# Adding the residual on POOL instead of VectorE at three normalised borders of a two-block fp32 kernel

## The chip, the core and the metric

The kernel runs on one core of one Trainium2 chip. The metric is the device time of one execution, in microseconds (us). TensorE is called PE here, its weight loads PEld, VectorE is DVE, ScalarE is ACT, GpSimd is POOL, and SyncE (SP) issues the DMAs.

## What is computed

`x` is 512 tokens of 1024 features in float32. The first block is a feed-forward, an attention mixture and a second feed-forward; each of them ends with a norm of its output and a residual add. A second block of two hybrid layers follows.

```python
def _rmsnorm(x, g):
    xf = x.astype(jnp.float32)
    r = lax.rsqrt(jnp.mean(xf * xf, axis=-1, keepdims=True) + EPS)
    return (xf * r * g.astype(jnp.float32)).astype(x.dtype)

# first_block
f = _swiglu(_rmsnorm(x, ffn1_pre_g[l]), ffn1_w_gate[l], ffn1_w_up[l], ffn1_w_down[l])
x = x + 0.5 * _rmsnorm(f, ffn1_post_g[l])            # border 1
h = _rmsnorm(x, mix_pre_g[l])
...
x = x + _rmsnorm(heads @ w_out[l], mix_post_g[l])    # border 2
f = _swiglu(_rmsnorm(x, ffn2_pre_g[l]), ffn2_w_gate[l], ffn2_w_up[l], ffn2_w_down[l])
x = x + 0.5 * _rmsnorm(f, ffn2_post_g[l])            # border 3
```

## The kernel before

The 512 tokens are four chunks of 128 tokens (`NC = 4`), one token per partition. Every matmul is done in three fp32r passes: each operand is split into a high part and a low part, and PE multiplies high by high, high by low and low by high (lines 1287 to 1289). Weights come as 326 slabs plus 8 extra ones, of 128 x 1024 floats each. A slab is loaded by SP, ACT casts it to its high part (`highs`, line 549), and POOL subtracts that from the raw slab to get the low part (`lows`, line 510, which writes `w_lo` or, for the extra slots, `x_lo`). PE waits for that low part before it uses a slab.

Between two stages stands a border. Border 1 lies between the first feed-forward and the qkv projection, border 2 between the mixture's output projection and the second feed-forward, border 3 between the second feed-forward and the first hybrid layer. At each of these three, and for each chunk `c` in turn, the two engines ACT and DVE hand the work to and fro:

- ACT squares and sums the product `f` of the chunk, which lies in two PSUM banks (`norm_f`, lines 555 and 556). DVE adds the two sums (line 858), ACT takes the root (line 559), DVE the reciprocal (line 860).
- DVE scales `f` by that and by the gain `g_post` into `xn` (line 867, two instructions, `new_x`), and adds `xn` to `x_tok` in place (line 870). That add raises `x_done`.
- ACT squares and sums the new `x_tok` (`norm_x`, line 569, which waits for `x_done`) and takes the root (line 570). DVE takes the reciprocal (line 881) and scales `x_tok` by it and by `g_pre` into `xn` (line 888, `normed`), which raises `xn_ready`.
- PE transposes `xn` (`turn_chunk`, line 1281). ACT copies the high part of the transposed chunk (`take_high`, line 576), DVE subtracts to get the low part (`take_low`, line 896), which raises `xtl_done`; then PE may multiply with that chunk.

Each engine's order is written out by hand and is strict. On DVE it is `new_x(c)`, `normed(c)`, `take_low(c-1)`; on ACT `norm_f(c)`, `norm_x(c)`, `take_high(c-1)`. Between `norm_x(0)` and `norm_f(1)` ACT casts two slabs of the next stage, those in the extra slots, and POOL makes their low parts. POOL has nothing else to do from there to the end of the border.

On PE the sums of the stage before end chunk by chunk (`out_product`), with the transposes of chunks 0 and 1 set after the sums of chunks 2 and 3. At borders 1 and 3 the next stage begins with `chunk_group`: for each chunk PE waits for `xtl_done` of this chunk, does 24 matmuls, and for the first two chunks then transposes chunk `c + 2`. At border 2 the next stage is `ffn`: its first matmuls wait for `xtl_done` of two chunks at once, then the transposes of chunks 2 and 3 come, and then a second wait for the other two chunks.

Of the kernel before, what the change touches and what calls it, by code (L numbers as in the profile page):

```python
# [8 lines left out]
ALU = mybir.AluOpType  # L9
# [8 lines left out]
NC = SEQ // P  # L18
# [7 lines left out]
LEAD = 4  # L26
# [15 lines left out]
S_QKV = N_IN + N_DOWN  # L42
S_OUT1 = S_QKV + N_QKV
# [79 lines left out]
def build(nc, x, ffn1_pre_g, ffn1_post_g, ffn1_w_gate, ffn1_w_up, ffn1_w_down, mix_pre_g, mix_post_g,  # L123
# [4 lines left out]
    with ExitStack() as ctx:  # L128
# [11 lines left out]
        def put(name, shape, dtype=F32):  # L140
            t = at(name, shape, dtype, place[0])
            place[0] += size(shape, dtype)
            assert place[0] <= arena_base + arena, (name, place[0] - arena_base - arena)
            return t


        x_tok = put("x_tok", [NC, D])
# [23 lines left out]
        xn = put("xn", [2, D])  # L171
# [78 lines left out]
        def f32(t):  # L250

            return t.bitcast(F32)
# [16 lines left out]
        def inv_sum(c):  # L269
            return col(96 + c)  # L270
# [13 lines left out]
        def factor2(par, comp=0, n=1):  # L284
            return col(114 + 2 * par + comp, n)
# [5 lines left out]
        def sem(name):  # L291
            return ctx.enter_context(nc.semaphore(name))
# [13 lines left out]
        acc_done = sem("acc_done")  # L306
        sqf_done, ssf_done, rtf_done = sem("sqf_done"), sem("ssf_done"), sem("rtf_done")
        x_done = sem("x_done")
        rtx_done = sem("rtx_done")
        xn_ready = sem("xn_ready")  # L310
        tr_done = sem("tr_done")
# [33 lines left out]
        def cols(c, n=P):  # L345
            return slice(c * n, (c + 1) * n)
# [4 lines left out]
        def stage_end(b):  # L351

            return {1: S_QKV, 2: S_FFN[1], 3: S_LAYER0, 4: S_LAYER0 + N_LAYER, 5: N_SLABS}[b]

        def wait_chunk_sums(eng, b, c):

            if c < NC - 1:
                eng.wait_ge(acc_done, 3 * (b - 1) + c + 1)
            else:
                eng.wait_ge(w_used, stage_end(b))  # L360

        def layer_start(l):
            return S_LAYER0 + l * N_LAYER
# [134 lines left out]
        @block.gpsimd  # L498
        def _(pool):
            pool.memset(ident[:, :], 0.0).then_inc(pool_step, 1)  # L500
            pool.wait_ge(pool_step, 1)
            pool.affine_select(out=ident[:, :], in_=ident[:, :], compare_op=ALU.not_equal, fill=1.0, base=0,
                               pattern=[[-1, P]], channel_multiplier=1).then_inc(ident_ready, 1)

            def lows(a, b):

                for s in range(a, b):
                    pool.wait_ge(hi_ready, s + 1)
                    i = slot_of[s]
                    pool.tensor_tensor(lo_slots[i], raw_slots[i], f32(hi_slots[i]), ALU.subtract).then_inc(lo_ready, 1)  # L510


            lows(0, S_OUT1 + LEAD)
            for i in range(16 * NC):
                pool.wait_ge(rd_done, i + 1)
                p = p_tok[:, i % NC, :]
                pool.tensor_scalar(p, p, inv_sum(i % NC), 1.0, ALU.mult, ALU.mult).then_inc(pn_done, 1)  # L517
            done = S_OUT1 + LEAD
            for l in range(LAYERS):
                upto = layer_start(l) + N_PROJ_A + LEAD  # L520
                lows(done, upto)
                done = upto
                for i in range(16):
                    n = 16 * l + i
                    w = (i % NC + 1) * P
                    pool.wait_ge(c2_done, n + 1)
                    p = p2[:, 2 * (n % 2), 0:w]
                    pool.tensor_scalar(p, p, factor2(n % 2), 1.0, ALU.mult, ALU.mult).then_inc(pw_done, 1)
            lows(done, N_SLABS)
# [314 lines left out]
        def _(dve):  # L844
            steps = [0]

            def link(ins):

                steps[0] += 1
                ins.then_inc(dve_step, 1)  # L850
                dve.wait_ge(dve_step, steps[0])

            def new_x(b, c):

                if b in (1, 2, 3):
                    n = 4 * (b - 1) + c + 1
                    dve.wait_ge(sqf_done, n)
                    dve.tensor_tensor(ss_f, ss_a, ss_b, ALU.add).then_inc(ssf_done, 1)
                    dve.wait_ge(rtf_done, n)
                    link(dve.reciprocal(inv_f, root_f))  # L860
                    if c == 0:
                        dve.wait_ge(post_in, 16 * b)
                    if 4 * b + c >= 2:
                        dve.wait_ge(tr_done, 4 * b + c - 1 if c >= 2 else 4 * b)
                    for half, bk in enumerate((bank[4 + c], bank[c])):
                        sl = cols(half, 512)
                        ins = dve.scalar_tensor_tensor(out=xn[:, c % 2, sl], in0=bk[:, :], scalar=inv_f,
                                                       in1=g_post[:, sl], op0=ALU.mult, op1=ALU.mult)
                    link(ins)
                    dve.tensor_tensor(x_tok[:, c, :], x_tok[:, c, :], xn[:, c % 2, :], ALU.add).then_inc(x_done, 1)  # L870
                elif b >= 4:
                    wait_chunk_sums(dve, b, c)
                    for half, bk in enumerate((bank[4 + c], bank[c])):
                        sl = cols(half, 512)
                        ins = dve.tensor_tensor(x_tok[:, c, sl], bk[:, :], x_tok[:, c, sl], ALU.add)  # L875
                    ins.then_inc(x_done, 1)
# [23 lines left out]
            def boundary(b):  # L900
                for c in range(NC):
                    new_x(b, c)
                    normed(b, c)
                    if c >= 1 and b < 5:
                        take_low(b, c - 1)
                if b < 5:
                    take_low(b, NC - 1)
# [85 lines left out]
            for c in range(NC):  # L993
                dve.wait_ge(qkv_evac, 16 + c + 1)
                ins = dve.tensor_tensor(v_hilo[:, c, 2:10, HD:P], bank[c][:, :].rearrange("p (h d) -> p h d", d=HD),
                                        f32(v_hilo[:, c, 2:10, 0:HD]), ALU.subtract)
# [77 lines left out]
            for l in range(LAYERS):  # L1074
# [60 lines left out]
                for i in range(17):  # L1135
                    n = 16 * l + i
                    h, c = i // NC, i % NC
# [86 lines left out]
                s = layer_start(l) + N_PROJ_A + N_PROJ_B  # L1224
# [20 lines left out]
                for jj in range(4):  # L1245
                    for b in range(3):
# [4 lines left out]
                        for jh in range(2):  # L1251
# [7 lines left out]
                            else:  # L1259
                                dve.tensor_tensor(m_tmp[:, :], src, g, ALU.mult).then_inc(gm_done, 1)  # L1260
                                dve.wait_ge(gm_done, 2 * n + jh + 1)
                                ins = dve.tensor_tensor(m_sum[:, jh, :], m_sum[:, jh, :], m_tmp[:, :], ALU.add)  # L1262
# [391 lines left out]
```

## Time and profile before

| | us |
|---|---|
| median of 3 runs | 2571.01 |
| lowest and highest of them | 2568.86, 2574.23 |
| the profiled execution | 2573.89 |
| its span in the profile | 2572.1 |
| PE busy in the span | 2303.0 (90%) |
| DVE busy | 762.4 (30%) |
| ACT busy | 801.3 (31%) |
| POOL busy | 870.3 (34%) |

The profiled execution is 2.88 us above the median and inside the spread of the others, so a difference worked out from its rows can be added to the median. PE is nearly full over the span; the other three engines are at a third. What an engine's operation is worth is thus decided by the few places at which PE waits for it.

### The profile page before, as it was taken

To read this page: it belongs to the slowest core of one execution; us is meant where nothing else is said; L and a number is where in the kernel's file an instruction comes from. 1 tells how busy PE (TensorE), PEld (TensorE's weight loads), DVE (VectorE), ACT (ScalarE), POOL (GpSimd) and SP (SyncE) were. 2 spreads that over 40 slices of the span, in tenths; PEclk is the share of its full clock that TensorE was granted. 3 is DMA by queue.
4 is the path that set the end of the run, shared out by engine and by line. 5 is a ranking of instruction groups with operands and counts; after the bars stand their busy time and mean duration, and the time that the engine had idled before them with its cause. 6 is when DMAs were issued, how large, how long until landed. Compare 5 with 4: busy or idle time off the path is not lost. (4 is left out here: it accounts for less than half of the span.)

```text
span 2572.1 us, 24728 instructions
## 1 busy us (share of the span) xinstructions
PE 2303.0 (90%) x10064; PEld 1873.7 (73%) x10064; DVE 762.4 (30%) x1411; ACT 801.3 (31%) x1391; POOL 870.3 (34%) x436
## 2 busy tenths in 40 slices
PE   5999999877667999999968879999997698799998
PEld 5888888755446888887747767888785587688886
DVE  2111006955653211103244333212124342331112
ACT  3222224244334322213334222222233332323222
POOL 3444443421113344443403303444442041144441
PEclk9999999966769999999957959999997597699999
DMA  4333333300002333322202202333231031033331
GB/s 139 98 94 95 98 107 116 90 1 0 1 1 65 91 99 98 98 92 97 86 1 75 89 1 78 94 98 98 82 111 33 33 91 41 25 99 94 95 98 66
DMA packets 231536, 190.94 MB, mean 74 GB/s; under 512 B 6400, under 2 KB 192256, under 8 KB 231168
## 3 DMA queue, kind: packets, MB, share of 16 engines
q1 hardware_dynamic: 231424, 189.37, 24.3%
q8 instruction: 80, 1.31, 0.2%
q14 instruction: 32, 0.26, 0.0%
HBM read 187.25 MB, written 2.10 MB: 74 GB/s over the span
## 5 line engine op out<-in xcount | busy, mean ns | idle before, releaser
L510 POOL TENSOR_TENSOR w_lo<-w_raw,w_hi 128x1024 fp32r<-128x1024 f32 x326 | 787.9, 2430 | 1245.3 <-ACT w_hi L549 1244.7
L1287 PE MATMUL bank<-xt_hi,w_hi 128*128 128x512 f32 (+1 forms) x1376 | 531.3, 386 | 17.9 <-DVE xt_lo L896 14.9
L1288 PE MATMUL bank<-xt_lo,w_hi 128*128 128x512 f32 (+1 forms) x1376 | 530.3, 385 | 0.0
L1289 PE MATMUL bank<-xt_hi,w_lo 128*128 128x512 f32 (+1 forms) x1376 | 529.6, 385 | 0.0
L549 ACT ACTIVATE w_hi<-w_raw 128x1024 fp32r<-128x1024 f32 x326 | 341.5, 1056 | 454.8 <-DMA w_raw<-in_w_in 203.9
L1287 PEld LDWEIGHTS bank<-xt_hi,w_hi 128*128 128x128 f32 x1376 | 263.1, 191 | 70.5 <-DVE xt_lo L896 16.0
L1288 PEld LDWEIGHTS bank<-xt_lo,w_hi 128*128 128x128 f32 x1376 | 263.2, 191 | 50.3
L1289 PEld LDWEIGHTS bank<-xt_hi,w_lo 128*128 128x128 f32 x1376 | 263.0, 191 | 50.4
L1287 PE MATMUL bank<-w_hi,xt_hi 128*128 128x512 f32 (+1 forms) x624 | 243.6, 390 | 4.1 <-DVE xt_lo L1042 2.8
L1288 PE MATMUL bank<-w_lo,xt_hi 128*128 128x512 f32 (+1 forms) x624 | 241.9, 388 | 0.0
L1289 PE MATMUL bank<-w_hi,xt_lo 128*128 128x512 f32 (+1 forms) x624 | 241.7, 387 | 0.0
L923 DVE TENSOR_TENSOR h_raw<-bank,act_gate 128x512 f32<-128x512 f32 x44 | 30.4, 692 | 399.9 <-PE bank L1289 399.9
L1287 PEld LDWEIGHTS bank<-w_hi,xt_hi 128*128 128x128 f32 x624 | 118.9, 190 | 29.7 <-DVE xt_lo L1042 3.2
L1288 PE MATMUL bank<-w_lo,h_hi 128*128 128x512 f32 x352 | 138.6, 394 | 0.0
L1287 PE MATMUL bank<-w_hi,h_hi 128*128 128x512 f32 x352 | 138.1, 392 | 0.0
L1289 PE MATMUL bank<-w_hi,h_lo 128*128 128x512 f32 x352 | 136.7, 388 | 0.0
L1289 PEld LDWEIGHTS bank<-w_hi,xt_lo 128*128 128x128 f32 x624 | 118.7, 190 | 23.9
L1288 PEld LDWEIGHTS bank<-w_lo,xt_hi 128*128 128x128 f32 x624 | 118.9, 191 | 23.3
L607 ACT ACTIVATE act_gate<-bank 128x512 f32<-128x512 f32 x44 | 26.3, 598 | 325.1 <-PE bank L1289 325.1
L517 POOL TENSOR_SCALAR p_tok<-p_tok,stat 128x512 f32<-128x512 f32 x64 | 44.3, 692 | 223.0 <-DVE stat L1015 222.7
L1287 PE MATMUL bank<-k_hi,q_hi 64*128 64x512 f32 (+3 forms) x128 | 59.6, 620 | 50.2 <-DVE k_lo L1004 30.4
L833 ACT ACTIVATE gate_sb<-bank 128x512 f32<-128x512 f32 x48 | 28.7, 598 | 198.6 <-PE bank L1289 198.6
(210 smaller groups left out, 3150.9 us busy)
## 6 DMA issues: line engine op xcount, KB each, us to landing
w_raw<-in_w_in SPq DMA_DIRECT2D x132, 512.0 KB, 3.8
w_raw<-in_ffn_w_down SPq DMA_DIRECT2D x44, 512.0 KB, 3.6
w_raw<-in_ffn_w_gate SPq DMA_DIRECT2D x43, 512.0 KB, 3.9
w_raw<-in_ffn_w_up SPq DMA_DIRECT2D x43, 512.0 KB, 3.8
w_raw<-in_w_out SPq DMA_DIRECT2D x24, 512.0 KB, 3.6
w_raw<-in_w_branch SPq DMA_DIRECT2D x24, 512.0 KB, 3.4
w_raw<-in_w_qkv SPq DMA_DIRECT2D x16, 512.0 KB, 3.8
x_tok<-in_x SPq DMA_DIRECT2D x4, 512.0 KB, 7.4
```

The lines of the kernel that those rows point to most:

```text
L510: pool.tensor_tensor(lo_slots[i], raw_slots[i], f32(hi_slots[i]), ALU.subtract).then_inc(lo_ready, 1)
L517: pool.tensor_scalar(p, p, inv_sum(i % NC), 1.0, ALU.mult, ALU.mult).then_inc(pn_done, 1)
L549: act.activation(hi_slots[i], raw_slots[i], ACT.Copy).then_inc(hi_ready, 1)
L607: act.activation(act_gate[:, f % 2, :], bank[gate_up_banks(f)[0]][:, :], ACT.Silu)\
L833: act.activation(gate_sb[:, jh, :], bank[b4 + jh][:, :], ACT.Sigmoid).then_inc(gs_done, 1)
L923: dve.tensor_tensor(h_raw[:, f % 2, :], bank[gate_up_banks(f)[1]][:, :], act_gate[:, f % 2, :], ALU.mult).then_inc(h_done, 1)
L1287: pe.matmul(out_ap, ah, bh, start=first, stop=False)
L1288: pe.matmul(out_ap, ah, bl, start=False, stop=False)
L1289: return pe.matmul(out_ap, al, bh, start=False, stop=last)
```

## The change

The residual add of borders 1, 2 and 3 goes from DVE to POOL. DVE's second scaling instruction (line 867) now raises a new semaphore `f_scaled`, in place of the link to the add behind it; POOL waits for `f_scaled`, adds, and raises `x_done`, for which ACT waits as before. In POOL's order the add of chunk 0 stands after the low parts of the first two slabs of the next stage, then come the low parts of the next two slabs (those in the extra slots), then the adds of chunks 1 to 3, and then the remaining low parts. The borders of the second block (`b >= 4`) are left alone.

```diff
+            def residual(b):
+
+                s = stage_end(b)
+                for c in range(NC):
+                    pool.wait_ge(f_scaled, 4 * (b - 1) + c + 1)
+                    pool.tensor_tensor(x_tok[:, c, :], x_tok[:, c, :], xn[:, c % 2, :], ALU.add).then_inc(x_done, 1)
+                    if c == 0:
+                        lows(s + 2, s + 4)
+
-            lows(0, S_OUT1 + LEAD)
+            lows(0, S_QKV + 2)
+            residual(1)
+            lows(S_QKV + 4, S_OUT1 + LEAD)
...
             done = S_OUT1 + LEAD
+            for b in (2, 3):
+                lows(done, stage_end(b) + 2)
+                residual(b)
+                done = stage_end(b) + 4
...
-                    link(ins)
-                    dve.tensor_tensor(x_tok[:, c, :], x_tok[:, c, :], xn[:, c % 2, :], ALU.add).then_inc(x_done, 1)
+                    ins.then_inc(f_scaled, 1)
```

The order of POOL around border 1, before. `w_lo` and `x_lo` are low parts of slabs, `p_tok` is the mixture's softmax:

```order
L510 TENSOR_TENSOR w_lo<-w_raw,w_hi 128x1024 [waits hi_ready] x68
L510 TENSOR_TENSOR x_lo_116<-x_raw_115,x_hi_117 128x1024 [waits hi_ready]
L510 TENSOR_TENSOR x_lo_119<-x_raw_118,x_hi_120 128x1024 [waits hi_ready]
L510 TENSOR_TENSOR w_lo<-w_raw,w_hi 128x1024 [waits hi_ready] x18
L517 TENSOR_SCALAR p_tok<-p_tok,stat 128x512 [waits rd_done] x64
```

The same place now:

```order
L511 TENSOR_TENSOR w_lo<-w_raw,w_hi 128x1024 [waits hi_ready] x68
L519 TENSOR_TENSOR x_tok<-x_tok,xn 128x1024 [waits f_scaled]
L511 TENSOR_TENSOR x_lo_116<-x_raw_115,x_hi_117 128x1024 [waits hi_ready]
L511 TENSOR_TENSOR x_lo_119<-x_raw_118,x_hi_120 128x1024 [waits hi_ready]
L519 TENSOR_TENSOR x_tok<-x_tok,xn 128x1024 [waits f_scaled] x3
L511 TENSOR_TENSOR w_lo<-w_raw,w_hi 128x1024 [waits hi_ready] x18
```

One add stands ahead of the two extra slabs and three behind them; the low parts keep their order among themselves.

The order of DVE at border 1, chunk 0 and the first steps of chunk 1, before:

```order
L858 TENSOR_TENSOR stat<-stat 128x1 [waits sqf_done]
L860 RECIPROCAL stat<-stat 128x1 [waits rtf_done]
L867 SCALAR_TENSOR_TENSOR xn<-bank,stat,g_post 128x512 [waits tr_done,post_in,dve_step]
L867 SCALAR_TENSOR_TENSOR xn<-bank,stat,g_post 128x512
L870 TENSOR_TENSOR x_tok<-x_tok,xn 128x1024 [waits dve_step]
L881 RECIPROCAL stat<-stat 128x1 [waits rtx_done]
L888 SCALAR_TENSOR_TENSOR xn<-x_tok,stat,g_pre 128x1024 [waits pre_in,dve_step]
```

The same place now:

```order
L874 TENSOR_TENSOR stat<-stat 128x1 [waits sqf_done]
L876 RECIPROCAL stat<-stat 128x1 [waits rtf_done]
L883 SCALAR_TENSOR_TENSOR xn<-bank,stat,g_post 128x512 [waits tr_done,post_in,dve_step]
L883 SCALAR_TENSOR_TENSOR xn<-bank,stat,g_post 128x512
L896 RECIPROCAL stat<-stat 128x1 [waits rtx_done]
L903 SCALAR_TENSOR_TENSOR xn<-x_tok,stat,g_pre 128x1024 [waits pre_in,dve_step]
```

The add is gone from DVE and nothing is put in its place: the next instruction after the scaling is still the reciprocal that waits for `rtx_done`. ACT, PE and SP keep their instructions and their order.

## Rows read from the trace of the kernel before

**Rows 1.** Timeline of DVE, border 1, chunk 2: start, duration, line, shapes [idle before]
```profile
401.14 1.41 DVE L867 SCALAR_TENSOR_TENSOR xn<-bank,stat,g_post 128x512 f32<-128x512 f32 x2
402.59 1.23 DVE L870 TENSOR_TENSOR x_tok<-x_tok,xn 128x1024 f32<-128x1024 f32 x1
...
405.47 1.28 DVE L888 SCALAR_TENSOR_TENSOR xn<-x_tok,stat,g_pre 128x1024 f32<-128x1024 f32 x1
406.67 1.28 DVE L896 TENSOR_TENSOR xt_lo<-bank,xt_hi 128x512 fp32r<-128x512 f32 x2
...
408.49 1.41 DVE L867 SCALAR_TENSOR_TENSOR xn<-bank,stat,g_post 128x512 f32<-128x512 f32 x2
```

**Rows 2.** Timeline of ACT, border 1, the same chunk
```profile
403.85 1.06 ACT L569 ACTIVATE junk<-x_tok 128x1024 bf16<-128x1024 f32 x1 [2.94 <-DVE x_tok L870]
...
405.03 0.20 ACT L570 ACTIVATE stat<-stat 128x1 f32<-128x1 f32 x1
```

**Rows 3.** Timelines of PE's weight loads and matmuls, border 1 (PEld) and both borders (PE)
```profile
399.47 0.86 PEld L1281 LDWEIGHTS bank<-ident,xn 128*128 128x128 f32 x8 [0.53 <-DVE xn L888]
400.66 0.19 PEld L1287 LDWEIGHTS bank<-w_hi,xt_hi 128*128 128x128 f32 x1 [0.34 <-DVE xt_lo L896]
406.80 0.85 PEld L1281 LDWEIGHTS bank<-ident,xn 128*128 128x128 f32 x8 [0.76 <-DVE xn L888]
...
414.15 1.09 PE L1281 MATMUL bank<-ident,xn 128*128 128x128 f32 x8 [0.32 <-DVE xn L888]
...
1220.59 1.09 PE L1281 MATMUL bank<-ident,xn 128*128 128x128 f32 x8 [0.32 <-DVE xn L888]
```

**Rows 4.** One line of the source each: durations in ns, least, median, most
```profile
L870 DVE TENSOR_TENSOR x_tok<-x_tok,xn x12: 1224/1225/1514, 386.6 to 1216.4; 128x1024 f32<-128x1024 f32 x12
...
L510 POOL TENSOR_TENSOR w_lo<-w_raw,w_hi x326: 2332/2402/2944, 11.0 to 2536.7; 128x1024 fp32r<-128x1024 f32 x163
...
L517 POOL TENSOR_SCALAR p_tok<-p_tok,stat x64: 691/691/696, 519.4 to 766.6; 128x512 f32<-128x512 f32 x64
```

**Rows 5.** Timelines in the mixture: DVE releases POOL; POOL's work; PEld released by POOL
```profile
702.66 0.16 DVE L1015 RECIPROCAL stat<-stat 128x1 f32<-128x1 f32 x1
...
702.92 0.69 POOL L517 TENSOR_SCALAR p_tok<-p_tok,stat 128x512 f32<-128x512 f32 x1 [10.33 <-DVE stat L1015]
...
522.60 0.69 POOL L517 TENSOR_SCALAR p_tok<-p_tok,stat 128x512 f32<-128x512 f32 x1 [0.59 <-DVE stat L1015]
...
523.65 0.71 PEld L1281 LDWEIGHTS bank<-ident,p_tok 128*128 128x128 f32 x4 [0.65 <-POOL p_tok L517]
```

**Rows 6.** Timelines of POOL, DVE and ACT, border 1, chunk 1
```profile
390.30 5.09 POOL L510 TENSOR_TENSOR x_lo<-x_raw,x_hi 128x1024 fp32r<-128x1024 f32 x2 [6.50 <-ACT x_hi L549]
417.39 5.21 POOL L510 TENSOR_TENSOR w_lo<-w_raw,w_hi 128x1024 fp32r<-128x1024 f32 x2 [22.00 <-ACT w_hi L549]
...
394.98 1.50 DVE L870 TENSOR_TENSOR x_tok<-x_tok,xn 128x1024 f32<-128x1024 f32 x1
...
396.51 1.06 ACT L569 ACTIVATE junk<-x_tok 128x1024 bf16<-128x1024 f32 x1 [3.21 <-DVE x_tok L870]
```

**Rows 7.** Timeline of PE, border 2
```profile
827.89 1.09 PE L1281 MATMUL bank<-ident,xn 128*128 128x128 f32 x8 [0.25 <-DVE xn L888]
836.42 0.58 PE L1287 MATMUL bank<-xt_hi,w_hi 128*128 128x256 f32 x1 [7.44 <-DVE xt_lo L896]
...
850.18 1.04 PE L1281 MATMUL bank<-ident,xn 128*128 128x128 f32 x8
853.72 0.58 PE L1287 MATMUL bank<-xt_hi,w_hi 128*128 128x256 f32 x1 [2.50 <-DVE xt_lo L896]
```

**Rows 8.** Stretches at border 2: length, then busy us of PE, PEld, DVE, ACT, POOL, granted clock, DMA
```profile
834.00:836.00 2.00, 0.00 (x0) 0.00 (x0) 2.00 (x3) 1.89 (x6) 0.00 (x0) 0.50 0.00 0
838.00:840.00 2.00, 2.00 (x13) 2.00 (x12) 1.53 (x2) 0.40 (x1) 0.00 (x0) 0.61 0.00 0
854.00:856.00 2.00, 2.00 (x10) 2.00 (x11) 0.00 (x0) 0.00 (x0) 0.00 (x0) 0.50 0.00 0
```

More of the change, by code:

```diff
@@ L308, in build @@
         x_done = sem("x_done")
+        f_scaled = sem("f_scaled")
         rtx_done = sem("rtx_done")
```

## The prediction

> **What bounds the kernel now.** I read the page first: PE is busy 90% of the span, so an operation of another engine costs only where PE waits for it. Then I read the timelines of the four engines over the three borders that the change touches. At border 1 the reader should follow one chunk round. DVE scales the product (401.14, 1.41 us) and adds it to x (402.59, 1.23 us) [rows 1]; 0.03 us later ACT squares the new x (403.85) and takes the root (405.03) [rows 2]; DVE makes xn (405.47, 1.28 us) and the low part of the chunk before (406.67, 1.28 us), and starts to scale the next chunk at 408.49 [rows 1]. That is a round of 408.49 - 401.14 = 7.35 us in which no two of the steps overlap. DVE sits in an ordered queue and can't use the time while ACT works. PE is a little faster than this round: its weight loads stand idle 0.53, 0.34 and 0.76 us for xn or for the low part, and the transposes of the last chunk still wait 0.32 us for xn, at border 3 as at border 1 [rows 3]. So at these borders the round of ACT and DVE sets the end, and PE has no spare time in front of it that could hide a longer round. At border 2 it is plainer: PE stands 7.44 us for the low part of chunk 1 and later 2.50 us for that of chunk 3 [rows 7].
>
> The add is a link of that round. It is 1.23 us between the scaling and ACT's squares, and all twelve adds take this except one of each border (1224 ns least, 1225 median, 1514 most) [rows 4].
>
> **What the change takes away.** From the end of the scaling (401.14 + 1.41 = 402.55) to the start of ACT's squares (403.85) the link is 1.30 us [rows 1, 2]. DVE has nothing to do with the time it is given: its next instruction waits for the root that ACT takes after the add. The freed DVE time is therefore worth nothing.
>
> **What it adds.** The same link is now: DVE releases POOL, POOL adds, POOL releases ACT.
>
> - DVE to POOL: a reciprocal ends at 702.66 + 0.16 = 702.82 and POOL starts at 702.92, after 10.33 us of idleness, so 0.10 us [rows 5].
> - The add. No row has POOL adding two float32 tiles. The nearest is its subtraction on the same 128x1024 shape with two float32 inputs: 2402 ns median, 2332 least [rows 4]. The far bound is its one-input operation, 691 ns on 512 elements, or 1.38 us on 1024 [rows 4]. I take 2.40, since the add has two inputs and the same size.
> - POOL to ACT: no row shows it. Bounds are the 0.03 us from DVE to ACT [rows 1, 2] and the only row in which an engine was released by POOL, PEld at 523.65 after a POOL operation that ended at 522.60 + 0.69 = 523.29, so 0.36 us at most [rows 5]. I take 0.10, as for the release in the other direction.
>
> Sum 0.10 + 2.40 + 0.10 = 2.60 us against 1.30, so **1.30 us more** for each of chunks 0, 2 and 3. POOL is idle there: it stands 22.00 us between the extra slabs and the next one [rows 6].
>
> The Trainium skill, GPSIMD Engine Reference, section "Performance versus the Vector engine", gives about 2.6 cycles per element for an elementwise operation of two inputs; at 1.2 GHz an estimate from that page for 1024 elements is 2.2 us, not 2.40. By the page the whole sum below would be about 2 us smaller. The rows of POOL's own subtraction decide here.
>
> Chunk 1 differs, because the two extra slabs stand ahead of it in POOL's queue. Before, POOL worked on them until 390.30 + 5.09 = 395.39, DVE's add (394.98) took 1.50 instead of 1.23 beside it, and ACT started at 396.51 [rows 6]. The slabs start from the same point of ACT's work as before, so in this chunk's own time they still end at 395.39; the scaling ended at about 394.94 and its release would reach POOL by 395.04, so the add starts at 395.39 and ACT at 395.39 + 2.40 + 0.10 = 397.89. That is **1.38 us more**. Behind the adds of chunks 1 to 3 in POOL's queue stand the low parts of the next slabs, and they wait for nothing new: their casts come on ACT only after its last step of the border.
>
> **What of it reaches the end.** Borders 1 and 3: the last wait of PE there is for xn of chunk 3, behind all four rounds [rows 3]. Delay 3 x 1.30 + 1.38 = 5.28 us each. Behind it PE does 24 matmuls and needs chunk 3's low part only at their end, which comes as far ahead as before. Border 2: the long wait ends with the low part of chunk 1, which DVE makes only after xn of chunk 2; so three rounds are in it, 2 x 1.30 + 1.38 = 3.98 us. The fourth is hidden: xn of chunk 3 is transposed at 850.18 behind work of PE without a wait, and the 2.50 us after that are counted from this transposition, so they stay [rows 7].
>
> Total 5.28 + 3.98 + 5.28 = 14.5 us. Slabs, casts, low parts and DMAs of the following stages are released by PE or come after the border on their engines, so everything behind moves as a block, and nothing there is late that was not.
>
> **PE's clock.** It falls to 0.50 in the 7.44 us wait and is 0.61 at 838 to 840, after which PE is at full clock; in the 2.50 us wait it falls again and is 0.50 at 854 to 856 [rows 8]. These are the two levels 1.2 and 2.4 GHz. About 2.8 us of PE's work ran at the low one after the first wait (836.42 to about 839.2), which cost some 1.4 us. Now the same wait is longer, and it costs that anyway. At borders 1 and 3 the wait for xn of chunk 1 grows from 0.53 to 0.53 + 1.30 + 1.38 = 3.2 us, more than the 2.50 that sufficed at border 2, so the clock may fall there. But each following round of PE now has 1.3 us to spare against the longer round of the others, which takes up most of such a 1.4 us. I put nothing into the sum and 0 to 1.4 us per border into the range.
>
> Against the profiled execution's 2573.89 us this is 2588.4; that execution lies 2.9 us above the median, so against the median 2571.01 it is 2585.5. **Forecast 2585.5 us**, 0.56% slower. The bounds of the unknowns: POOL's release at 0.03 or at 0.36 us moves it by 11 x -0.07 = -0.8 or 11 x 0.26 = +2.9 us; the add at its least, 2332 ns, by -0.8; the clock by up to +4.2; the scatter of the runs by about 2 either way.
>
> **Rivals.**
>
> 1. The add at POOL's one-input pace. If a plain float32 add ran at 1.38 us [rows 4] rather than 2.40, a round would grow by 0.28 instead of 1.30, and chunk 1 by 0.36: 2 x 1.20 + 0.92 = 3.3 us, 2574.3 us, within 0.2% and so not slower by what can be told. It decides from an add of about 1.6 us down; below 1.1 us (1.30 less the two releases) the kernel would even become faster. For it: nothing but the missing row. Against it: the subtraction reads the same two kinds of input. Chance 0.05, of which 0.01 for faster.
> 2. A low clock at borders 1 and 3 that isn't taken up, for instance because it falls in the last waits, behind which no wait of PE is left, or because border 2 starts longer at 1.2 GHz than before. Price 1.4 us each at three or four places, with the forecast's 14.5: 2589 to 2592, say 2590. For it: the clock fell after 2.50 us of waiting [rows 8]. Against: at border 1 waits of 0.3 to 0.8 us did not pull it down, and the new ones after chunk 1 are 1.6 to 2.1 us. Chance 0.15.
> 3. The delay is hidden, in that PE's waits of 0.3 us at borders 1 and 3 are only the edge of the record and PE itself is the limit with 1 us to spare per round. Then only 0.3 of each 1.3 us would count there: about 3 + 4 = 7 us, 2578 us. Against it: PE's waits repeat in each round, each named as waiting for DVE. Chance 0.05.
>
> **How the numbers follow.** Forecast with its own range 2581 to 2589: 0.75. Rival 1: 0.05, rival 2: 0.15, rival 3: 0.05. A measurement of this kernel can tell about 0.2%, 5 us, from no change. Slower by more: 0.95; within: 0.04, which is rival 1; faster: 0.01. The range reaches over rival 2: 2580 to 2592 us.
>
> **What would show it.** In the profile of the changed kernel: POOL's adds at 2.4 us, ACT's idle time before its squares at about 4.2 us instead of 2.94, a round of 8.65 us instead of 7.35, PE's wait before the second transposes of border 1 at about 3.2 us and before the later ones at about 1.6 to 2.1, the long wait of border 2 at 7.44 + 1.3 = 8.7 us (the rest of its 3.98 stands before the transposes). The stage behind each border should be as long as before. An add under 2 us, or a round still at 7.4 us, would refute the first step; a PE that doesn't wait longer would refute the second; a stage behind the border that is shorter or longer would mean that I missed what moves with it.

## The result

The changed kernel takes 2586.73 us (median of 5 runs, 2586.30 to 2587.95); the kernel before, now with five runs, 2573.24 us (2568.86 to 2575.41). The ratio is **1.0056**, with a 95% interval of 1.0041 to 1.0070: slower by 13.5 us from median to median, by some 11 to 18 us by the interval. The profiled execution of after took 2586.73 us with a span of 2584.9.

The line of the page after with the busy time of each engine answers to the table of before:

```profile
PE 2304.6 (89%) x10064; PEld 1873.9 (72%) x10064; DVE 746.8 (29%) x1399; ACT 801.2 (31%) x1391; POOL 898.2 (35%) x448
```

DVE loses 12 instructions and 15.6 us, POOL gains 12 and 27.9 us, and PE does the same work in a longer span.

The line of the new add in the source view (durations in ns, least, median, most; below it, who waited for whom, in us and times) answers to [rows 4]:

```profile
L519 POOL TENSOR_TENSOR x_tok<-x_tok,xn x12: 2337/2392/2409, 386.3 to 1228.4; 128x1024 f32<-128x1024 f32 x12
...
  DVE xn L883: 45.2, 9
...
  ACT junk L585: 50.8, 12
```

The add costs 2.39 us on POOL, and ACT waits for all twelve, 50.8 us together; it was 36.1 us for DVE's.

The timeline of chunk 2 of border 1, DVE, POOL and ACT, answers to [rows 1, 2]:

```profile
403.32 1.41 DVE L883 SCALAR_TENSOR_TENSOR xn<-bank,stat,g_post 128x512 f32<-128x512 f32 x2
...
408.64 0.16 DVE L896 RECIPROCAL stat<-stat 128x1 f32<-128x1 f32 x1 [3.91 <-ACT stat L586]
...
411.86 1.41 DVE L883 SCALAR_TENSOR_TENSOR xn<-bank,stat,g_post 128x512 f32<-128x512 f32 x2
...
404.81 2.38 POOL L519 TENSOR_TENSOR x_tok<-x_tok,xn 128x1024 f32<-128x1024 f32 x1 [6.16 <-DVE xn L883]
...
407.22 1.06 ACT L585 ACTIVATE junk<-x_tok 128x1024 bf16<-128x1024 f32 x1 [4.14 <-POOL x_tok L519]
```

Read it in order of time. DVE's scaling ends at 404.73 and POOL starts at 404.81, 0.08 us later. POOL ends at 407.19 and ACT starts at 407.22, 0.03 us later. The link is 2.49 us where it was 1.30, and the round is 411.86 - 403.32 = 8.54 us where it was 7.35. DVE meanwhile stands idle 3.91 us: the time it was given is spent waiting.

PEld (first line) and PE at borders 1 and 2 answer to [rows 3, 7]:

```profile
401.64 1.42 PEld L1296 LDWEIGHTS bank<-ident,xn 128*128 128x128 f32 x8 [3.04 <-DVE xn L903]
...
401.64 1.82 PE L1296 MATMUL bank<-ident,xn 128*128 128x128 f32 x8 [2.61 <-DVE xn L903]
410.18 1.10 PE L1296 MATMUL bank<-ident,xn 128*128 128x128 f32 x8 [0.27 <-DVE xn L903]
...
418.73 1.09 PE L1296 MATMUL bank<-ident,xn 128*128 128x128 f32 x8 [1.51 <-DVE xn L903]
...
846.07 0.58 PE L1302 MATMUL bank<-xt_hi,w_hi 128*128 128x256 f32 x1 [8.60 <-DVE xt_lo L911]
...
863.26 0.39 PE L1302 MATMUL bank<-xt_hi,w_hi 128*128 128x256 f32 x1 [2.50 <-DVE xt_lo L911]
```

PE's wait before the second transposes of border 1 is 2.61 us, before the last 1.51, and the long wait of border 2 is 8.60 instead of 7.44. The 3.2 us forecast for the first of them started from the 0.53 us of PEld, and PEld's wait is 3.04; PE itself had a gap of only 0.10 us there before, which its rows don't list as a wait.

The timelines give the length of each stretch between two events. At borders 1 and 3 I take it from the scaling of chunk 0 (the start of DVE's first scaling) to PE's transposes of chunk 3, at border 2 from the same scaling to PE's first matmul behind the long wait. In the kernel before these are 414.15 - 385.18 = 28.97, 836.42 - 813.59 = 22.83 and 1220.59 - 1191.63 = 28.96 us.

| stretch of the profiled execution | before | after | difference |
|---|---|---|---|
| start to border 1 | 385.18 | 384.84 | -0.34 |
| border 1 | 28.97 | 33.89 | +4.92 |
| qkv and mixture | 399.44 | 400.89 | +1.45 |
| border 2 | 22.83 | 26.45 | +3.62 |
| rest of border 2, second feed-forward | 355.21 | 353.84 | -1.37 |
| border 3 | 28.96 | 33.90 | +4.94 |
| rest of the span | 1351.51 | 1351.09 | -0.42 |
| span | 2572.1 | 2584.9 | +12.8 |

The three borders take 13.48 us more; everything else together changes by -0.7 us. That the medians differ by the same 13.5 us is partly chance, since their interval is some 7 us wide; the borders are the surer figure.

### The profile page after: what moved, and what is told of

It reads as the page before. It is cut to its first block and busy times, and to the rows that moved or that the text cites. A ratio compares the mean times of both kernels' runs of the same rounds, so it can differ in the third digit from the quotient of the medians.

```text
span 2584.9 us, 24728 instructions
## 1 busy us (share of the span) xinstructions
PE 2304.6 (89%) x10064; PEld 1873.9 (72%) x10064; DVE 746.8 (29%) x1399; ACT 801.2 (31%) x1391; POOL 898.2 (35%) x448
```

## The experiments

Nine runs of seven kernels. The sum of the three border stretches is the finer measure: it repeats from execution to execution within 0.05 us where a border is left alone, while single executions of one kernel differ by over 10 us. Each run shared its chip with runs of the kernel before.

| run | ratio to before (95%) | border 1 | border 2 | border 3 | sum of the three, against before |
|---|---|---|---|---|---|
| before | | 28.97 | 22.83 | 28.96 | |
| the change | 1.0056 (1.0041 to 1.0070) | 33.89 | 26.45 | 33.90 | +13.48 |
| POOL at border 2 only | 1.0017 (1.0002 to 1.0032) | 28.96 | 26.43 | 28.97 | +3.60 |
| POOL at borders 1 and 3 only | 1.0050 (1.0032 to 1.0068) | 33.87 | 22.83 | 33.90 | +9.84 |
| longer link on DVE | 1.0062 (1.0044 to 1.0081) | 33.78 | 26.35 | 33.78 | +13.15 |
| no add | 0.9968 (0.9955 to 0.9980) | 26.87 | 18.76 | 26.86 | -8.27 |
| DVE adds, early parts | 0.9985 (0.9972 to 0.9999) | 27.20 | 18.70 | 27.22 | -7.64 |
| the same again | 0.9979 (0.9968 to 0.9989) | 27.19 | 18.69 | 27.19 | -7.69 |
| POOL adds, early parts | 1.0011 (0.9995 to 1.0027) | 31.51 | 20.35 | 31.51 | +2.61 |
| shared add | 1.0032 (1.0018 to 1.0045) | 29.66 | 23.45 | 29.62 | +1.97 |
| the same again | 1.0014 (1.0003 to 1.0025) | 29.64 | 23.45 | 29.64 | +1.97 |

### One part of the change at a time

```diff
             for b in (2, 3):          # border 2 only: (2,), and border 1 as before
-                    ins.then_inc(f_scaled, 1)
+                    if b in (2,):     # the other kernel: (1, 3)
+                        ins.then_inc(f_scaled, 1)
+                    else:
+                        link(ins)
+                        dve.tensor_tensor(x_tok[:, c, :], x_tok[:, c, :], xn[:, c % 2, :], ALU.add).then_inc(x_done, 1)
```

> POOL adds the residual at border 2 only; at borders 1 and 3 VectorE adds as before. My theory (each add lengthens its round by about 1.2 us, chunk 1's by 1.3, and PE's long wait of border 2 has three rounds in it): 3.7 us over the kernel before, ratio 1.0014, PE's wait after the transposes of chunk 1 at border 2 near 8.6 us, borders 1 and 3 unchanged (28.97 us from the scaling of chunk 0 to the transposes of chunk 3). Rival (all four adds of a border count, wherever they stand): 4.9 us, a third of the whole change's 13.5.

> POOL adds at borders 1 and 3 only. My theory: 4 rounds each, 3 x 1.20 + 1.30 = 4.9 us per border, 9.8 us over the kernel before, ratio 1.0038; with the kernel that has only border 2 changed it sums to the 13.5 us of the whole change. Rival (the fall of PE's clock at borders 1 and 3 costs time of its own): the two parts don't sum, or these two borders take over 5.5 us each. Rival (the clock spells of the attention stages are dealt anew): any sum, with no pattern by border.

Border 2 alone costs 3.60 us, borders 1 and 3 alone 4.90 and 4.94; the sum, 13.44, is that of the whole change (13.48), and the borders left alone keep their length to 0.01 us. The rival of four counted adds at border 2 (4.9 us) is out by the stretch, though not by the time: 1.0017 has 1.0019 in its interval. The excesses of the two ratios sum to 0.0067, and their intervals leave room for the 0.0056 of the whole change.

### A longer link without POOL

```diff
                     link(ins)
+                    for half, bk in enumerate((bank[4 + c], bank[c])):
+                        sl = slice(512 * half, 512 * half + 432)
+                        ins = dve.scalar_tensor_tensor(out=xn[:, c % 2, sl], in0=bk[:, 0:432], scalar=inv_f,
+                                                       in1=g_post[:, sl], op0=ALU.mult, op1=ALU.mult)
+                    link(ins)
                     dve.tensor_tensor(x_tok[:, c, :], x_tok[:, c, :], xn[:, c % 2, :], ALU.add).then_inc(x_done, 1)
```

> The kernel before, with VectorE's add kept, and 2 x 432 columns of the scaling done a second time in front of it (same values), which makes the same link about 1.2 to 1.25 us longer with POOL out of it. My theory (only the length of the round counts, not who adds): 4 x 1.23, 3 x 1.23, 4 x 1.23 = 13.5 us over the kernel before, the same time as the changed kernel within 0.1%. Rival (part of the cost is POOL's own: its queue, its releases, its hold on what VectorE shares with it): clearly less, 8 us or under.

DVE at border 1, the first scalings of chunks 2 and 3:

```profile
403.65 1.41 DVE L867 SCALAR_TENSOR_TENSOR xn<-bank,stat,g_post 128x512 f32<-128x512 f32 x2
...
412.27 1.41 DVE L867 SCALAR_TENSOR_TENSOR xn<-bank,stat,g_post 128x512 f32<-128x512 f32 x2
```

This is a round of 8.62 us with DVE alone, against 8.54 with POOL. The borders are 13.15 us longer, of the 13.5 expected, and the time is 1.0062, beside 1.0056 of the change. Chunk 1 accounts for what is missing: its round grew by 1.00 us and the others by 1.27, because the add there now comes behind POOL's two slabs and takes 1.22 us, not 1.50. It is the length of the link that costs, not the engine that holds it. The rival (8 us or less) falls. PE's clock fell here too, to a mean of 0.70 from 404 to 408, after a wait of 2.36 us; so that fall isn't POOL's doing either.

### How far PE is behind

```diff
-                    link(ins)
-                    dve.tensor_tensor(x_tok[:, c, :], x_tok[:, c, :], xn[:, c % 2, :], ALU.add).then_inc(x_done, 1)
+                    ins.then_inc(x_done, 1)
```

> The residual add of borders 1 to 3 is left out (x stays what it was); the scaling releases ScalarE's squares. The link loses 1.26 us per chunk. My theory (PE is just behind the round and becomes the limit at borders 1 and 3, where it needs 24 matmuls and the transposes, about 6.6 us against a round of 6.1): 1.6 us gained at each of borders 1 and 3 and 3.8 at border 2, 7 us in all, ratio 0.9973. Rival (PE is far from the limit): 5.0 + 3.8 + 5.0 = 13.8 us gained, ratio 0.9946. Rival (PE already limits at borders 1 and 3): 3.8 us, ratio 0.9985.

This kernel leaves the add out altogether. The timeline of DVE has the round at 6.07 us now, that of PE (lower two lines) has the transposes 6.41 us apart and without a wait:

```profile
397.06 1.41 DVE L867 SCALAR_TENSOR_TENSOR xn<-bank,stat,g_post 128x512 f32<-128x512 f32 x2
...
403.13 1.41 DVE L867 SCALAR_TENSOR_TENSOR xn<-bank,stat,g_post 128x512 f32<-128x512 f32 x2
...
404.34 1.04 PE L1280 MATMUL bank<-ident,xn 128*128 128x128 f32 x8
410.75 1.03 PE L1280 MATMUL bank<-ident,xn 128*128 128x128 f32 x8
```

Borders 1 and 3 gain 2.10 each and border 2 gains 4.07, 8.27 together; I had expected 1.6 and 3.8. Both rivals fall: neither is PE the limit already nor far from it. It is 7.35 - 6.41 = 0.94 us per round behind the round of the others. That is the asymmetry at borders 1 and 3: what lengthens the round counts in full, what shortens it counts for 0.94 us a round at most.

### Using DVE's idle time by another order

The chunk before is finished earlier: ACT copies its high part before it waits for the new x, and DVE subtracts its low part while ACT squares. The same lines stand in ACT's `boundary` with `take_high` and `norm_x`.

```diff
                     new_x(b, c)
+                    early = b in (1, 2, 3) and c >= 1 and (b, c) != (2, 3)
+                    if early:
+                        take_low(b, c - 1)
                     normed(b, c)
-                    if c >= 1 and b < 5:
+                    if c >= 1 and b < 5 and not early:
                         take_low(b, c - 1)
```

> The kernel before (VectorE adds), with the high and low parts of chunk c-1 taken earlier in chunk c: ScalarE's copy stands before its squares of the new x instead of behind them, VectorE's subtraction between the add and the reciprocal (chunk 3 of border 2 excepted). It then runs while VectorE waits 1.45 us for ScalarE. My theory (VectorE's idle time in a round is only worth something if a step of the round is moved into it): the round falls by 1.2 us to under PE's 6.4, so PE limits borders 1 and 3 (1.8 us gained each), and the low part that ends the long wait of border 2 comes 4.0 us sooner. Together 7.6 us under the kernel before, ratio 0.997. Rival (the two engines have no gap that fits, so the steps only change places): no change, 1.000.

The timeline of DVE, border 1, chunk 2 (starts and durations as above):

```profile
399.28 1.41 DVE L870 SCALAR_TENSOR_TENSOR xn<-bank,stat,g_post 128x512 f32<-128x512 f32 x2
400.72 1.23 DVE L873 TENSOR_TENSOR x_tok<-x_tok,xn 128x1024 f32<-128x1024 f32 x1
401.86 1.28 DVE L899 TENSOR_TENSOR xt_lo<-bank,xt_hi 128x512 fp32r<-128x512 f32 x2
403.40 0.16 DVE L884 RECIPROCAL stat<-stat 128x1 f32<-128x1 f32 x1 [0.25 <-ACT stat L570]
...
405.42 1.41 DVE L870 SCALAR_TENSOR_TENSOR xn<-bank,stat,g_post 128x512 f32<-128x512 f32 x2
```

DVE's idle time before the reciprocal falls from 1.45 to 0.25 us, since the subtraction lies in it, and the round from 7.35 to 6.14. The borders gain 7.64 us, of the 7.6 expected. The time showed less, 0.9985 (4 us), hence a second measurement:

> The early parts with VectorE adding once more. Its borders were 1.77, 4.13 and 1.75 us shorter, 7.65 us together (ratio 0.997); the time measured was 0.9985 (0.9972 to 0.9999). If the borders' gain reaches the end, the ratio comes back between 0.9965 and 0.9985 with the borders as before; if part of it is given back in a later stage, the ratio stays near 0.9985 and that stage is longer in the profile.

It gave 0.9979 (0.9968 to 0.9989) with the same stretches, -7.69. The stage between borders 2 and 3 is 1186.15 - 830.60 = 355.55 us against 355.21 before, so nothing is given back there. The interval takes in the 7.7 us of the borders (0.9970). This kernel beats both: it is some 5 us faster than the one before by the medians (4.8 and 6.1 us), and 7.6 by the borders.

> The changed kernel (POOL adds), with the same earlier high and low parts. VectorE's subtraction now lies beside POOL's add. My theory: the round is 8.54 - 1.20 = 7.34 us, as long as before the change; borders 1 and 3 take 2.5 us longer than in the kernel before (4.9 in the changed one), border 2 takes 2.5 us less: 2.5 us over the kernel before, ratio 1.001, and 10 us slower than the same order with VectorE adding. Rival (once VectorE's freed time is used, the change pays): faster than the early order with VectorE adding. Rival (the subtraction beside POOL's add is held up by it): the round stays near 8.5 us, ratio 1.005.

With POOL adding, DVE's subtraction lies beside the add, and the round is 409.82 - 402.47 = 7.35 us, as before the change. DVE, then ACT, border 1, chunk 2:

```profile
402.47 1.41 DVE L886 SCALAR_TENSOR_TENSOR xn<-bank,stat,g_post 128x512 f32<-128x512 f32 x2
404.93 1.29 DVE L914 TENSOR_TENSOR xt_lo<-bank,xt_hi 128x512 fp32r<-128x512 f32 x2 [1.05 <-ACT xt_hi L592]
...
409.82 1.41 DVE L886 SCALAR_TENSOR_TENSOR xn<-bank,stat,g_post 128x512 f32<-128x512 f32 x2
...
403.81 1.08 ACT L592 ACTIVATE xt_hi<-bank 128x512 fp32r<-128x512 f32 x2 [1.57 <-PE bank L1302]
406.39 1.06 ACT L585 ACTIVATE junk<-x_tok 128x1024 bf16<-128x1024 f32 x1 [1.49 <-POOL x_tok L519]
```

The borders take 2.61 us more than in the kernel before (2.5 expected) and 10.25 more than the same order with DVE adding. Even when DVE has work for the time it is given, that work fits into the time it had anyway, and the slower add stays in the round. Both rivals fall: the change doesn't pay here either, and the subtraction is not held up by POOL (the two L914 instructions take 1.29 us beside POOL's add, and 1.28 without it in [rows 1]).

### Sharing the add between the two engines

```diff
-                    pool.tensor_tensor(x_tok[:, c, :], x_tok[:, c, :], xn[:, c % 2, :], ALU.add).then_inc(x_done, 1)
+                    pool.tensor_tensor(x_tok[:, c, 0:512], x_tok[:, c, 0:512], xn[:, c % 2, 0:512], ALU.add)\
+                        .then_inc(p_added, 1)
...
+                        if half == 0:
+                            ins.then_inc(f_scaled, 1)
+                    link(ins)
+                    dve.tensor_tensor(x_tok[:, c, 512:D], x_tok[:, c, 512:D], xn[:, c % 2, 512:D], ALU.add)\
+                        .then_inc(x_done, 1)
```

> The add is shared: POOL adds columns 0 to 511 as soon as VectorE has scaled them, VectorE scales and then adds columns 512 to 1023; ScalarE waits for both. The traces show VectorE's operations with two SBUF inputs stretched while POOL works (1.50 instead of 1.23 us, 0.57 instead of 0.15). My theory (VectorE's half add can't run until POOL's is done): POOL's half takes 1.2 us, VectorE's record starts beside it and ends 0.6 us behind it, the link is 1.95 us from the first half's scaling against 1.99 in the kernel before, and the time is that of the kernel before, ratio 1.000. Rival (they run side by side): VectorE's half add takes 0.65 us, the link is 0.58 shorter, 5 us gained, ratio 0.998.

DVE, POOL and ACT at border 1, chunk 2, and POOL at chunk 1 (last line):

```profile
400.87 1.41 DVE L887 SCALAR_TENSOR_TENSOR xn<-bank,stat,g_post 128x512 f32<-128x512 f32 x2
402.32 1.23 DVE L892 TENSOR_TENSOR x_tok<-x_tok,xn 128x512 f32<-128x512 f32 x1
...
401.70 1.30 POOL L520 TENSOR_TENSOR x_tok<-x_tok,xn 128x512 f32<-128x512 f32 x1 [5.54 <-DVE xn L887]
...
403.58 1.06 ACT L589 ACTIVATE junk<-x_tok 128x1024 bf16<-128x1024 f32 x1 [2.94 <-DVE x_tok L892]
...
394.41 1.75 POOL L520 TENSOR_TENSOR x_tok<-x_tok,xn 128x512 f32<-128x512 f32 x1
```

Half an add takes DVE as long as a whole one did, 1.23 us. POOL is done at 403.00, DVE at 403.55, which is 0.55 us later and near half of a whole add's 1.23. So the two did not run side by side, and DVE's row seems to hold its waiting for POOL. ACT's idle time is 2.94 us as in [rows 2]. The shared add gains nothing in chunks 0, 2 and 3, and costs 0.66 us in chunk 1, where POOL's half stands behind the extra slabs; this cost I had not expected. The rival (5 us gained) falls. The Trainium skill, SBUF — State Buffer, section "SBUF: two separate sides", calls the ports that the two engines share an exclusive lock, held for a whole instruction against a VectorE operation with two SBUF inputs; this row agrees with it.

The ratio of 1.0032 is 8 us more (0.0032 of 2570) where the borders show 2, hence a second measurement:

> The shared add once more. Its borders took 0.69, 0.62 and 0.66 us more than in the kernel before, 2.0 us together, all of it in chunk 1, where POOL's half stands behind the two extra slabs; the time measured was 8 us more (1.0018 to 1.0045). If the rest was the way in which PE's low clock happened to fall in the attention stages, the ratio comes back nearer to 1.001 and the borders show 2.0 us again. If the shared add costs something outside the borders, it stays at 1.003 and a stage in the profile is longer by 6 us.

It gave 1.0014 with the same 1.97 us in the borders, and its interval (1.0003 to 1.0025) takes in the 2 us (1.0008). So most of the first excess did not come back; the part between border 1 and border 2 differs from one execution to the next, as the last section shows. That nothing at all is left outside the borders isn't shown.

## Why the prediction was right

**The bound and the link.** The round of ACT and DVE sets the end of all three borders. That a longer link counts in full was borne out with POOL and with DVE alone.

**The size of a step.** I had 1.30 us per add and 1.38 for chunk 1. Measured from the end of the scaling to ACT's squares it is 2.49 - 1.30 = 1.19, and for chunk 1, from 395.81 to 398.68, 2.87 - 1.57 = 1.30. The add itself was right (2.40 guessed, 2.39 measured). Too large were the two releases: 0.08 into POOL instead of 0.10, and above all 0.03 out of it where I had taken 0.10 between bounds of 0.03 and 0.36. POOL releases ACT as fast as DVE does. Eight rounds at 0.11 and three at 0.08 us make 1.1 us, the difference between the 14.5 us of the sum and the 13.5 of the borders.

**The time itself.** The forecast of 2585.5 us is 1.2 below the 2586.73 measured, and that is closer than the steps deserve. The sum was 1.1 us too large, and the median it was added to, 2571.01 of three runs, is 2.2 us below the 2573.24 of five. The two errors have opposite signs, which is luck; what held is the mechanism, to 0.1 us per round.

**Which rounds count.** Four at borders 1 and 3 (5.28 forecast, 4.92 and 4.94 measured), three at border 2 (3.98 forecast, 3.62 measured). Changing one part at a time showed the borders to be independent of each other.

**PE's clock.** The wait before the second transposes of borders 1 and 3 did bring the clock down, as I had left open. Stretches of after, the first two at border 1, then border 3, then the two waits of border 2 (length, busy us of PE, PEld, DVE, ACT and POOL, granted clock):

```profile
400.00:404.00 4.00, 2.36 (x10) 2.27 (x11) 3.56 (x8) 2.51 (x8) 0.00 (x0) 0.73 0.06 20
404.00:408.00 4.00, 4.00 (x16) 3.19 (x16) 0.73 (x2) 0.78 (x1) 2.38 (x1) 0.84 0.00 0
1216.00:1222.00 6.00, 5.23 (x20) 4.11 (x21) 3.49 (x7) 1.58 (x6) 2.13 (x1) 0.72 0.35 117
846.00:850.00 4.00, 3.93 (x22) 3.93 (x23) 1.66 (x5) 0.20 (x1) 1.96 (x1) 0.63 0.02 4
863.00:867.00 4.00, 3.74 (x31) 3.74 (x32) 0.21 (x1) 0.74 (x3) 0.00 (x0) 1.00 0.02 4
```

At border 1 PE's second transposes took 1.82 us instead of 1.09, and its next wait was 0.27 us, where the last round had 1.51. At border 3 the fall came a little later (the transposes took 1.14), and no wait is listed before the next ones. The low clock was paid out of time in which PE had to wait anyway, and each border is 4.9 us longer, no more.

Border 2 is less settled. The clock was low when the long wait ended, as before. In this execution it was high again after the second wait of 2.50 us (863 to 867 at 1.00, where [rows 8] have 0.50), and the stage behind was 1.37 us shorter. In the kernel with only border 2 changed, whose border 2 is the same, it went the other way:

```profile
829.00:833.00 4.00, 3.23 (x15) 3.23 (x16) 2.36 (x6) 0.47 (x3) 1.26 (x1) 0.50 0.02 4
833.00:837.00 4.00, 4.00 (x24) 4.00 (x24) 1.41 (x2) 1.35 (x3) 1.11 (x1) 0.62 0.00 0
849.00:853.00 4.00, 4.00 (x24) 4.00 (x23) 0.00 (x0) 0.00 (x0) 0.00 (x0) 0.58 0.01 4
```

Its long wait ended at 829.77 and the clock was still low for most of 833 to 837; it fell once more behind the second wait, which ended at 848.43, and the same stage took 1186.56 - 829.77 = 356.79 us, 1.58 more than before. So the term that I put at zero is zero at borders 1 and 3, and between -1.4 and +1.6 us at border 2 by these two profiles. That it came out below zero in the profile of the change is luck. My working of the old cost was also a little short: 0.61 over 838 to 840 [rows 8] means 1.56 us at the lower level, so the clock rose at about 839.6 and not 839.2, and about 3.1 us of PE's work had run at it.

**The rivals.** An add at POOL's one-input pace (rival 1) is out: 2337 ns is the least of the twelve. A clock that isn't taken up (rival 2) is out at borders 1 and 3; what it says of border 2 did happen in one profile, as above, at a price of 1.58 us. Hidden waits (rival 3) are out by the part experiments. PE does have 0.94 us to spare per round, as rival 3 had it, but that spare time lies behind the others' round, where it shortens nothing and hides nothing.

## What to carry to other kernels

Before an operation is moved to an idle engine, look whether it lies in a chain in which the engines wait for each other in turn: there only its own length and its releases count. In this case it counted for nothing how idle the engine was that took it or how busy the one that gave it. The price here was (new length - old length) times the rounds in front of the last wait. A gap in such a chain is used not by taking work out of it but by moving a later step of the round into it, as the earlier low part did here. Where the effect is a few us in a program whose single executions differ by more, measure the stretch between two named events.

## What was not expected

The executions of one kernel differ by some 15 us (the kernel before: 2560.6 to 2575.8 in 23 runs), and the profiles put most of it in one stage. Between the transposes of chunk 3 at border 1 and the first scaling of border 2, the mixture took 399.44 us in the profile of before and 803.34 - 414.08 = 389.26 in that of the kernel with only border 2 changed, though nothing in it differs. Stretches of before, then of that kernel:

```profile
510.00:800.00 290.00, 209.65 (x715) 140.95 (x716) 150.18 (x370) 111.97 (x213) 52.50 (x68) 0.70 0.01 4
860.00:1180.00 320.00, 320.00 (x1437) 265.34 (x1436) 32.92 (x44) 83.49 (x104) 148.11 (x62) 1.00 0.32 96
```

```profile
510.00:800.00 290.00, 209.01 (x761) 141.90 (x762) 150.25 (x370) 114.29 (x215) 56.31 (x70) 0.75 0.03 10
860.00:1180.00 320.00, 320.00 (x1415) 264.40 (x1414) 32.22 (x43) 82.58 (x103) 145.97 (x61) 1.00 0.32 94
```

In the mixture PE has many short waits and its clock goes to and fro between its levels, with a mean of 0.70 here and 0.75 there (single microseconds of before read 0.50 at 540 and 1.00 at 560). Of the eleven profiles, the two with a mean of 0.75 over 510 to 800 took 389.3 and 390.3 us for this stage, the nine with 0.68 to 0.71 took 396.9 to 401.2. In the middle of the feed-forward behind it the clock is 1.00 in both; that stage, border 2's second wait included, took 353.8 to 356.8, and all behind border 3 took 1349.6 to 1352.2. So the clock and the length of the mixture go together. That the one causes the other isn't shown, and what decides which way an execution goes was not tried.

A whole add is 2.39 us on POOL and half of it 1.30, so by these two sizes about 0.2 us of each instruction don't depend on its size. Splitting such work finely would, by this estimate, cost more than the halves suggest.
